# Hybrid trunk on one core: key, value and first gate columns side by side, and an earlier second input of the state scan

## What is computed

```python
for l in range(DEPTH):      # DEPTH = 2, SEQ = 256, D_MODEL = 1024, D_FF = 2816
    x = layer_norm(ALPHA * x + 0.5 * swiglu(x, ffn1_w_gate[l], ffn1_w_up[l], ffn1_w_down[l]), ...)
    x = layer_norm(ALPHA * x + hybrid_mixer(x, w_in[l], ...), ...)
    x = layer_norm(ALPHA * x + 0.5 * swiglu(x, ffn2_w_gate[l], ffn2_w_up[l], ffn2_w_down[l]), ...)
```

## Time and profile before

| what | value |
|---|---|
| median of 3 runs | 1126.09 us (1125.82 to 1126.22) |
| the profiled execution's own time | 1126.29 us |
| its span, first to last instruction | 1124.7 us |
| mean granted TensorE clock | 0.996 of full speed |
| TensorE, VectorE, ScalarE busy | 98%, 65%, 51% |
| chain that ended last, by engine | TensorE 87%, VectorE 8% |

### The profile page before, as it was taken

One profiled execution on the slowest core, in us unless ns is written; L12 is line 12 of the kernel. 1 busy time (PEld: TensorE's weight loads), 2 busy tenths in 40 slices (PEclk: granted clock), 3 DMA queues, 4 the chain that ended last, 5 costly groups with the idle time before them and its releaser, 6 DMA issues.

```text
span 1124.7 us, 14761 instructions
## 1 busy us (share of the span) xinstructions
PE 1101.4 (98%) x5591; PEld 917.7 (82%) x5591; DVE 736.5 (65%) x721; ACT 577.0 (51%) x646; POOL 126.3 (11%) x137
## 2 busy tenths in 40 slices
PE   9999999999899999999999999999998999999997
PEld 6888888998687788888877888889986877888885
DVE  4755447789878774544677554576979777644446
ACT  4755554767454443433466555546764436343341
POOL 1495000000000000000005940000000000000000
PEclk9999999999999999999999999999999999999999
DMA  8755567355275365556556555665344664655550
GB/s 256 247 187 186 186 214 198 122 179 191 93 213 204 133 224 186 186 186 215 197 152 203 191 196 180 232 168 187 118 155 127 210 225 129 221 194 193 181 203 37
DMA packets 163200, 205.39 MB, mean 183 GB/s; under 512 B 28228, under 2 KB 133336, under 8 KB 163160
## 3 DMA queue, kind: packets, MB, share of 16 engines
q1 hardware_dynamic: 163160, 204.84, 55.6%
HBM read 203.77 MB, written 1.05 MB: 182 GB/s over the span
## 4 chain that ended last, share of the span: by engine, by line
PE 87%; DVE 8%; issue 2%; ACT 2%; POOL 0%; POOLq 0%; DVEq 0%; ACTq 0%
PE ps L519 20%; PE ps L496 16%; PE ps L498 16%; PE ps L497 16%; PE ps L480 2%; PE ps L481 2%; PE ps L482 2%; PE ps L604 2%; DVE w_lo L1283 1%; PE ps L834 1%; PE ps L833 1%; PE ps L832 1%; PE ps L488 1%; PE ps L489 1%; PE ps L490 1%
## 5 line engine op out<-in xcount | busy, mean ns | idle before, releaser
L1283 DVE TENSOR_TENSOR w_lo<-raw,w_hi 128x2048 fp32r<-128x2048 f32 x174 | 402.8, 2320 | 194.2 <-ACT w_hi L916 193.8
L916 ACT CAST w_hi<-raw 128x2048 fp32r<-128x2048 f32 x174 | 332.1, 1912 | 174.0 <-PE ps L498 131.6
L496 PE MATMUL ps<-w_hi,xT 128*128 128x512 f32 x832 | 330.5, 397 | 8.8 <-DVE w_lo L1283 8.8
L498 PE MATMUL ps<-w_hi,xT 128*128 128x512 f32 x832 | 325.1, 391 | 0.0
L497 PE MATMUL ps<-w_lo,xT 128*128 128x512 f32 x832 | 324.6, 390 | 0.0
L496 PEld LDWEIGHTS ps<-w_hi,xT 128*128 128x128 f32 x832 | 156.7, 188 | 43.3 <-DVE w_lo L1283 11.4
L498 PEld LDWEIGHTS ps<-w_hi,xT 128*128 128x128 f32 x832 | 156.5, 188 | 33.7
L497 PEld LDWEIGHTS ps<-w_lo,xT 128*128 128x128 f32 x832 | 156.9, 189 | 31.1
L519 PE MATMUL ps<-w_hi,rows_hi 128*128 128x512 f32 x416 | 134.1, 394 | 2.3 <-DVE rows_lo L1676 1.3
L519 PE MATMUL ps<-w_hi,rows_lo 128*128 128x512 f32 x416 | 132.4, 390 | 0.0
L519 PE MATMUL ps<-w_lo,rows_hi 128*128 128x512 f32 x416 | 132.2, 390 | 0.0
(11 more groups left out here) (218 smaller groups left out, 1191.9 us busy)
## 6 DMA issues: line engine op xcount, KB each, us to landing
raw<-in_ffn_w_down SPq DMA_DIRECT2D x44, 1024.0 KB, 4.7
raw<-in_ffn_w_gate SPq DMA_DIRECT2D x87, 512.0 KB, 3.8
raw<-in_ffn_w_up SPq DMA_DIRECT2D x87, 512.0 KB, 4.7
raw<-in_w_in SPq DMA_DIRECT2D x34, 1024.0 KB, 5.0
raw<-in_w_out SPq DMA_DIRECT2D x8, 1024.0 KB, 4.7
raw<-in_w_in SPq DMA_DIRECT2D x16, 256.0 KB, 4.4
raw<-in_w_br_attn SPq DMA_DIRECT2D x8, 512.0 KB, 6.1
gb<-in_ln_g SPq DMA_DIRECT2D x6, 512.0 KB, 5.5
```

The lines of the kernel that those rows point to most:

```text
L496: mm(o, xT[:, c, 0, tok], h, start=c == UPPER_FIRST[0], stop=False, skip_group_check=True)
L498: return mm(o, xT[:, c, 1, tok], h, start=False, stop=c == UPPER_FIRST[-1], skip_group_check=True)
L916: nc.scalar.copy(w_hi[s][:, :], raw[s][:, :]).then_inc(hi_made.sem, 1)
L1283: tt(w_lo[s][:, :], raw[s][:, :], f32(w_hi[s][:, :]), ALU.subtract).then_inc(lo_made.sem, 1)
```

## The change

KV and GS become two chunks of the same 512 columns, keys, values and gates side by side: the first holds the upper half of the contraction (row blocks 4 to 7), the second the lower half. `first_products` uses `gate_up` with 512 moving columns into banks 0 and 1, two loads fill each chunk, and ScalarE reads keys and values after both. TensorE's order in the mixer's middle changes: S0's transposes directly behind S1's, then `gates_upper(1)`, output and input states, `attend(1)`, `gates_lower(1)`; `gates_upper(4)` ahead of `attend(0)`, and `gates_lower(4)` ahead of the GLU. ScalarE and VectorE follow. In the tail `lo(24)` goes behind the sums' remainders. `ahead(0)` goes ahead of the residual of tile 1 in every norm that has a next stage, and norm 1's second chunk has its remainders ahead of the norm. In the second layer's first FFN `scaled_back` goes behind step 2. At the start the first chunk's upper rows come in two parts with a load, cast and remainder each, tile 1's transposes go ahead of the second products, and the third chunk's load ahead of the small vectors.

```diff
-for _k in ATTN + CONV_SSM:
+for _k in ATTN + CONV_SSM + (KV, GS):
     DMAS[MIX0 + _k] = 2
...
-            for n in range(2):
-                sp.dma_start(paired(raw[0])[:, 0:2, n * 256:n * 256 + 256], first[n][:, 4:6, 0:256]
-                             ).then_inc(first_landed, 16)
+            for c in range(2):
+                for n in range(2):
+                    sp.dma_start(paired(raw[0])[:, c, n * 256:n * 256 + 256], first[n][:, 4 + c, 0:256]
+                                 ).then_inc(first_landed[c], 16)
...
+                load(l, k0 + 2, gate_up(w_gate, w_up, l, 1, 256))
                 after_two()
-                load(l, k0 + 2, gate_up(w_gate, w_up, l, 1, 256))
...
+            def first_columns(l, upper):
+                def parts(r):
+                    for n, c0 in enumerate((OFF_K, OFF_G)):
+                        yield paired(r)[:, :, n * 256:n * 256 + 256], at_layer(w_in, l).rearrange(
+                            "(c p) n -> p c n", p=P)[:, 4 * upper:4 * upper + 4, c0:c0 + 256]
+                return parts
...
-                pe.wait_ge(first_lo, 1)
-                first_gate_up(0, -1, 0, 0)
+                pe.wait_ge(x_lo.sem, x_lo.at(0, -8 + 1))
+                for c in PAIRS[0]:
+                    pe.wait_ge(first_lo, c - 3)
+                    gate_up(first_w_hi, first_w_lo, 0, c, 0)
+                transposes(0, -1, 1)
                 take(0, 0)
                 first_gate_up(0, -1, 0, 1)
-                transposes(0, -1, 1)
...
+                    hi, lo = (kv_w_hi, kv_w_lo) if p < 2 else (w_hi[0], w_lo[0])
                     for c in PAIRS[p]:
-                        kv = by_token(t, c, kv_w_hi, kv_w_lo, ps[:, t, 0:SEQ])
-                        gs = by_token(t, c, w_hi[0], w_lo[0], ps[:, 2 + t, 0:SEQ])
+                        last = gate_up(hi, lo, t, c, t)
...
-                pe.wait_ge(proj_read.sem, proj_read.at(l, 1))
+                pe.wait_ge(proj_read.sem, proj_read.at(l, GS + 1))
...
                 transpose_probs(S1, 4, 0)
-                gates_upper(1)
-                gates_lower(1)
                 pe.wait_ge(probs_made.sem, probs_made.at(l, 2))
                 transpose_probs(S0, 2, 4)
-                attend(1)
+                gates_upper(1)
+                pe.wait_ge(pT_made.sem, pT_made.at(l, 6))
                 output_states(0)
                 input_states(1)
+                attend(1)
+                gates_lower(1)
...
                 gates_lower(3)
+                gates_upper(4)
                 pe.wait_ge(ya_lo.sem, ya_lo.at(l, 1))
                 attend(0)
                 output_states(1)
-                gates_upper(4)
+                gates_lower(4)
...
                 last.then_inc(glu_done.sem, 1)
-                gates_lower(4)
...
                 probs_out(0, 4)
+                probs_out(4, 2)
                 split(l, MIX0 + 13)
+                states(2)
+                attn_hi(1, 1)
                 split(l, MIX0 + 14)
+                states(3)
                 gate(1, 0)
                 gate(1, 1)
-                probs_out(4, 2)
-                attn_hi(1, 1)
-                states(2)
                 split(l, MIX0 + 15)
-                states(3)
...
                     second(1)
+                    ahead(0)
                     residual_stats(1, 0, acc(3))
-                    ahead(0)
...
-                    if l:
-                        scaled_back(l, -1)
-                    else:
+                    if not l:
                         dve.sem_inc(x_made.sem, 1)
                     discretise()
 
-                second_tile = ffn(l, 0, early, input_matrices)
+                second_tile = ffn(l, 0, early, input_matrices, (lambda: scaled_back(l, -1)) if l else None)
...
-                attn_rest(1, 1)
                 turn_in(2)
                 lo(14)
+                attn_rest(1, 1)
                 scan(2)
+                lo(15)
                 turn_out(2)
-                lo(15)
+                lo(16)
                 turn_in(3)
-                lo(16)
+                lo(17)
                 scan(3)
                 turn_out(3)
-                lo(17)
+                lo(18)
...
                 gated(4, 2, 1, chunk_done(ATTN[1]))
-                lo(24)
                 gated(5, 0, 1, (conv_done.sem, conv_done.at(l, 2)))
                 sum_rest(0)
                 sum_rest(1)
+                lo(24)
...
-                norm(l, 1, FFN0[1] - 1, 1.0, rest_halves(l, 2))
+                second = rest_halves(l, 2)
+                second(0)
+                second(1)
+                norm(l, 1, FFN0[1] - 1, 1.0, lambda lower: None)
```

More of the change, by code:

```diff
@@ L922, in split_halves @@
                 sc_.wait_ge(used.sem, used.at(l, k - 1 - SLOTS + 1))
-                halves = (slice(0, CHUNK // 2), slice(CHUNK // 2, CHUNK))
-                for n, made in zip(halves[::-1] if stage == 1 else halves, (second_hi, hi_made)):
+                for n, made in ((slice(0, CHUNK // 2), second_hi), (slice(CHUNK // 2, CHUNK), hi_made)):
                     nc.scalar.copy(w_hi[0][:, n], raw[1][:, n]).then_inc(made.sem, 1)
@@ L1027, in turn_input @@
                 cast(0, 1)
-                sc_.wait_ge(first_landed, 32)
-                nc.scalar.copy(paired(first_w_hi)[:, 0:2, :], paired(raw[0])[:, 0:2, :]).then_inc(first_hi, 1)
-                cast(0, 0)
+                for c in range(2):
+                    sc_.wait_ge(first_landed[c], 32)
+                    nc.scalar.copy(paired(first_w_hi)[:, c, :], paired(raw[0])[:, c, :]).then_inc(first_hi, 1)
                 sc_.wait_ge(landed[0], LANDED[0])
                 nc.scalar.copy(paired(first_w_hi)[:, 2:4, :], paired(raw[0])[:, 2:4, :]).then_inc(hi_made.sem, 1)
+                cast(0, 0)
                 cast(1, 1)
@@ L1337, in ffn @@
                     early()
-                with dve.Fori(2, STEPS - 1) as i:
+                if second_step:
+                    step(2)
+                    second_step()
+                with dve.Fori(3 if second_step else 2, STEPS - 1) as i:
                     step(i)
@@ L1477, in turn_input @@
                 low(0, 1)
-                dve.wait_ge(first_hi, 1)
-                tt(paired(first_w_lo)[:, 0:2, :], paired(raw[0])[:, 0:2, :], f32(paired(first_w_hi)[:, 0:2, :]), ALU.subtract
-                   ).then_inc(first_lo, 1)
-                low(0, 0)
+                for c in range(2):
+                    dve.wait_ge(first_hi, c + 1)
+                    tt(paired(first_w_lo)[:, c, :], paired(raw[0])[:, c, :], f32(paired(first_w_hi)[:, c, :]), ALU.subtract
+                       ).then_inc(first_lo, 1)
                 dve.wait_ge(hi_made.sem, hi_made.at(0, 1))
@@ L1484, in turn_input @@
                    ).then_inc(lo_made.sem, 1)
+                low(0, 0)
                 low(1, 1)
```

45 lines of the change are left out of this document (21 added, 24 removed).

## The result

The changed kernel takes 1112.19 us (median, 1111.48 to 1113.17) against 1126.15 for the kernel before, measured beside it: a ratio of 0.9874 [0.9862, 0.9886]. The forecast was 1111.2, with a range of 1108.5 to 1117.5. The profiled execution took 1111.48 with a span of 1109.7 (before: 1126.29 and 1124.7), so 15.0 of span went.

The account below looks back on a forecast made before the run. TensorE, busy 98% of the span, bounds the kernel, so gains are its waits, slow running or removed matmul time. Terms -11.4 - 1.7 - 1.1 - 0.8 + 2.0 - 1.9 = -14.9 gave 1111.2 us, range 1108.5 to 1117.5.

Parts of the forecast that it names:

- Middle: Mixer's middle: reordering removes both TensorE remainder waits, half clock and slow restarts; 6.4 and 5.0 us by layer, -11.4.
- the slack of four us: Mixer's middle: remainders 14 to 17 end four us before TensorE needs them, 18 three us before.
- Output projection: Ahead of the output projection: chunk 24's remainder moved behind gating and sum remainders removes a wait; -0.85 per layer, -1.7.
- FFN: Second layer's first FFN: xtok scalings moved behind step 2 remove a 0.94 us wait and its slow restart; -1.1.
- Columns: Key, value and gate products: 96 matmuls of 256 columns become 48 of 512 per layer; -0.4 each, -0.8.
- Norms: Five norms: x_rest(0,0) ahead of tile 1's residual delays tile 1's transposes; +0.4 each, +2.0.
- Second chunk's halves ahead of norm 1: FFN's second chunk: both halves ahead of norm 1 sit in VectorE idle time; nothing.
- Start: Kernel start: split casts and remainders let tile 1's first matmul begin at 12.15 for 14.07; -1.9, bounds 0 and -1.9.
- slower by the clock: Rival: clock falls to 1.2 GHz behind closer transposes, state and attention matmuls; five chunks at low level give 1138; chance 0.03.
- two more issues per chunk: 512-column chunk loads: two more DMA issues would lose 2 us each in series; 512 KB pieces overlap, so given no share.

Follow-up runs that it names:

- the two slack runs: Changed kernel plus 2.4 us, or 7.15 us, of extra VectorE rotation products ahead of the second input's rotation in each layer: 1111.78 us and 1120.32 us.
- the middle alone: Kernel before with only the mixer's middle reordered on TensorE, ScalarE and VectorE; start, norms, columns, FFN and tail as before: 1113.86 us, ratio 0.9888.
- the tail run: Changed kernel with `scaled_back` in the discretisation again and `lo(24)` ahead of the fifth branch's gating and the sum's remainders: 1114.63 us, ratio 0.9902.
- the kernel with three extra pairs: Changed kernel with three extra pairs of rotation products (7.15 us) on VectorE ahead of the second input's rotation in each layer: 1120.32 us, ratio 0.9947.

## Why the prediction was right, and where it was not

- **Middle**, -11.4 foreseen, -12.46 by the marks. First layer 6.4 for 6.49 (the terms as listed add to 6.5); the second was mis-sized, 5.0 for 5.97. Before, that layer has the same two waits and then two more, 0.18 at 860.72 and 0.47 at 868.99, where the sum has one short wait at about 0.1; the rest is slow steps that I priced too low. The places and the slack of four us were right, which the two slack runs confirm. What the prediction lacks is a price for each part: it recovered the 1.90 us of idling and moved the remainders in one count. By the waits, the sooner input removes the two long ones of before. The new order of the last gate pair asks for remainders 17 and 18 sooner, and with these in their old places the kernel is slower than before (1127.7 with all other edits in, for 1126.1). So the remainders' new places are what the gates' new order needs; how much each part would give without the others is not shown. The two prices, 7.8 a layer for the places and 1.06 for 4.2 us of the input, are each taken from the whole change and don't add up to it.
- **Output projection** -1.7: 0.84 ahead of `w_out` twice, -1.68. In the plain marks it shows as -1.24 only, since the middle alone makes the step ahead of `w_out` 0.21 longer in each layer.
- **FFN** -1.1: -1.26. Nothing waits for the moved scalings.
- **Columns** -0.8: 0.5 by the run with 256 columns; the step that failed is that all 96 matmuls were taken to be on the path. The marks of the change show only -0.14 there (-0.08 and -0.06). The moved remainder takes 0.16 of the difference (with it put back, these steps are 0.07 and 0.09 shorter); the other 0.2 stays open.
- **Norms** +2.0: +1.64 by the marks of the change, 1.8 by the medians and 2.0 by the marks of the run without the edit. The mechanism is as told, the count a little off. The chain from residual to normalisation is 4.46 now, not 4.84, since the remainder has left it, while the residual starts 0.87 later (555.69, for 562.32 less 7.50), not the 0.53 from which the sum counts; together 0.49 for 0.53.
- **Second chunk's halves ahead of norm 1**, costed at nothing: about -0.3 a layer. Before, tile 0's transposes of norm 1 start 0.27 behind their pitch; after they don't. I name the halves as the cause by elimination from the marks (-0.38 and -0.42, of which the tail run takes 0.10); no run isolates it.
- **Start** -1.9: -0.59. The failed step is the assumption that equal bytes land at equal times: tile 1 lands 2.35 later and the second chunk's up half 1.9 later than before. The bound of 0 covered it. With the load whole and only the casts split it is -1.75. Of the later landings 0.93 is the later issue; what makes the rest stays open.

The sum came out at -14.84 for -14.9 because misses cancelled, which is luck: by the marks the start (+1.3), the columns (+0.7) and the output projection (+0.5) against the middle (-1.1), the step ahead of norm 1 (-0.8), the norms (-0.4) and the FFN (-0.2). The rival "slower by the clock" expected a fall behind the closer transposes, state and attention matmuls; behind 24 transposes in a row the clock reads 1.00. The falls read here stand behind stops of TensorE, as in the run with the remainders' old places.

The Trainium skill, "DMA: Bandwidth & Descriptors", section "Rules for kernel authors", which asks for at least 1 MiB a DMA and which the prediction gave no share, pointed the right way at the start: with pieces of 256 KB for 128 KB the kernel was 1.6 us faster by the medians, 0.55 by the profiled executions. The 2.0 us fixed stand in that page's section "Anatomy of one DMA — SWDGE (gpsimd) path", as a fit for DMAs issued from GpSimd, while these are issued from SyncE; in series they would have made two more DMAs 4 us, an estimate from the page's figure, and the landings behind them came 1.1 later. The prediction's "two more issues per chunk" should read one more: each of the two chunks goes from one load to two.

## What to carry to other kernels

Before moving the producer of a late input, write down for each piece of the busy helper engine when it ends and when it is needed: here the second input could come 4 us later for 1 us a layer, and beyond that slack each further us cost about one. When the bottleneck's order is changed, redo the helper's order for it too: with the new gate order, four remainders one place further back in VectorE's queue cost 7.8 us a layer, at chunks that had no wait before. To tell what each part of a reordering gives, look at which wait goes and which one is new, not at the total alone. At this kernel's start, split casts and remainders helped and split loads didn't. And a piece put ahead of a chain because it is ready soon delays the chain by its own wait: look at who is ready first to the tenth of a microsecond.

## What the runs showed of the hardware

- A stop of TensorE alone doesn't tell what the clock does. In the kernel before, the window behind the stops of 1.59 and 2.50 us reads 0.76 in the first layer, and behind the same stops in the second layer it reads 1.00. Behind one stop of 2.45 us the granted clock stayed at 1.00 in the first layer of the kernel with three extra pairs, and the window of 7 us behind the same stop in its second layer reads 0.80:

```profile
292.00:299.00 7.00, 7.00 (x31) 5.80 (x32) 7.00 (x8) 1.88 (x3) 0.00 (x0) 1.00 0.59 164
...
844.00:851.00 7.00, 7.00 (x26) 5.67 (x25) 6.97 (x8) 1.51 (x3) 0.00 (x0) 0.80 0.69 228
```

- Two DMAs of 256 KB in four pieces moved the landings of the 512 KB transfers behind them by 1.0 and 1.1 us (0.5 to 1.2 over eight traces), and the later issue alone is 0.93; issuing on SyncE, 0.4 to 0.5 us a DMA, took up to 2.40 when the third chunk was asked for early.
- Two matmuls of 256 moving columns take 0.01 us more than one of 512 (0.24 a pair against 0.227).
